# A two-layer diffusion step with top-2 experts on one core: expert rows weighted on the way out of PSUM, the second gather summed by its transfer, and TensorE fillers with a halved shift in the router

## What is computed

```python
def _moe(h, m, P):
    logits = jnp.einsum('nd,de->ne', xf, P['router'][m], preferred_element_type=jnp.float32)
    probs = jax.nn.softmax(logits, axis=-1)
    top_p, top_i = lax.top_k(probs, TOP_K)
    top_p = top_p / jnp.sum(top_p, axis=-1, keepdims=True)
    gates = jnp.sum(jax.nn.one_hot(top_i, N_EXPERTS, dtype=jnp.float32) * top_p[..., None], axis=1)
    for e in range(N_EXPERTS):
        y = y + gates[:, e:e + 1].astype(xf.dtype) * _swiglu(
            xf, P['moe_w_gate'][m, e], P['moe_w_up'][m, e], P['moe_w_down'][m, e])
# in _layer:  x = x + gf * f      and after the last layer:  y = _rmsnorm(x, final_norm_g)
```

## Time and profile before

| | us |
|---|---|
| median of 3 runs (1997.52 to 1998.13) | 1997.91 |
| the profiled execution's own time | 1998.52 |
| its span, first to last instruction | 1996.9 |
| TensorE busy in the span | 1971.9 (99%) |
| VectorE busy | 1530.0 (77%) |
| ScalarE busy | 1136.3 (57%) |
| GpSimd busy | 258.3 (13%) |

### The profile page before, as it was taken

How to read it: one execution, slowest core, us unless ns; L and a number is a source line. 1 busy time by engine, 2 the same in 40 slices (tenths; PEclk the granted TensorE clock), 3 DMA queues, 4 the chain that set the end, 5 groups by cost and what they waited for, 6 DMA issues and landing times. The chain is left out here.

```text
span 1996.9 us, 31145 instructions
## 1 busy us (share of the span) xinstructions
PE 1971.9 (99%) x11754; PEld 1763.4 (88%) x11754; DVE 1530.0 (77%) x1696; ACT 1136.3 (57%) x1383; POOL 258.3 (13%) x261
## 2 busy tenths in 40 slices
PE   8999999999999999999999999999999999999997
PEld 5898689999999999999879988888888888888885
DVE  5548678877767775765853589998998989989998
ACT  5217663322212223532865468777888887788775
POOL 1230100000000000132100056000000000000016
PEclk9999999999999999999999999999999999999999
DMA  9320433344444443422003499999999999999994
GB/s 336 99 86 6 149 117 127 127 138 153 153 149 143 152 135 98 128 67 74 1 1 74 174 346 374 385 386 386 386 384 384 386 386 383 381 385 385 385 378 190
DMA packets 265150, 448.21 MB, mean 224 GB/s; under 512 B 15104, under 2 KB 156384, under 8 KB 264896
## 3 DMA queue, kind: packets, MB, share of 16 engines
q1 hardware_dynamic: 244496, 378.37, 53.9%
q0 software_dynamic: 18688, 66.27, 9.1%
q10 hardware_dynamic: 1872, 2.26, 0.3%
HBM read 431.34 MB, written 16.64 MB: 224 GB/s over the span
## 5 line engine op out<-in xcount | busy, mean ns | idle before, releaser
L2102 DVE TENSOR_TENSOR w_lo<-mraw,w_hi 128x1792 fp32r<-128x1792 f32 (+2 forms) x306 | 643.7, 2116 | 80.6 <-ACT w_hi L1381 79.0
L1381 ACT ACTIVATE w_hi<-mraw 128x1792 fp32r<-128x1792 f32 (+2 forms) x306 | 541.4, 1775 | 166.0 <-PE ps L2788 161.6
L2786 PE MATMUL ps<-w_hi,xs_lo 128*128 128x448 f32 (+1 forms) x816 | 309.6, 379 | 0.7 <-DVE xs_lo L2107 0.7
L2788 PE MATMUL ps<-w_hi,xs_hi 128*128 128x448 f32 (+1 forms) x816 | 304.9, 374 | 0.0
L2787 PE MATMUL ps<-w_lo,xs_hi 128*128 128x448 f32 (+1 forms) x816 | 304.5, 373 | 0.0
L1503 DVE TENSOR_TENSOR sub_lo<-zone,sub_hi 128x1024 fp32r<-128x1024 f32 (+2 forms) x112 | 129.4, 1157 | 117.1 <-ACT sub_hi L1036 116.7
L1036 ACT ACTIVATE sub_hi<-zone 128x1024 fp32r<-128x1024 f32 (+2 forms) x112 | 109.2, 977 | 176.8 <-PE ps L2378 93.7
L2786 PEld LDWEIGHTS ps<-w_hi,xs_lo 128*128 128x128 f32 x816 | 153.2, 188 | 24.9 <-DVE w_lo L2102 6.4
L2788 PEld LDWEIGHTS ps<-w_hi,xs_hi 128*128 128x128 f32 x816 | 153.2, 188 | 19.2
L2787 PEld LDWEIGHTS ps<-w_lo,xs_hi 128*128 128x128 f32 x816 | 153.4, 188 | 17.8
L2363 PE MATMUL ps<-f_hi,sub_lo 128*128 128x320 f32 x704 | 162.2, 312 | 0.0
(11 more groups left out here) (360 smaller groups left out, 3653.0 us busy)
## 6 DMA issues: line engine op xcount, KB each, us to landing
mraw<-in_moe_w_down SPq DMA_DIRECT2D x68, 1024.0 KB, 8.9
mraw<-in_moe_w_up SPq DMA_DIRECT2D x68, 896.0 KB, 8.3
mraw<-in_moe_w_gate SPq DMA_DIRECT2D x68, 896.0 KB, 8.4
in_cos<-in_w_mods POOLq DMA_DIRECT2D x72, 512.0 KB, 3.6
mraw<-in_moe_w_gate SPq DMA_DIRECT2D x34, 1024.0 KB, 7.1
mraw<-in_moe_w_up SPq DMA_DIRECT2D x34, 1024.0 KB, 8.2
mraw<-in_moe_w_down SPq DMA_DIRECT2D x34, 768.0 KB, 8.5
zone<-in_w_in SPq DMA_DIRECT2D x13, 1024.0 KB, 5.2
```

The costliest lines, as they stand in the source:

```text
L1381: nc.scalar.activation(w_hi[:, n % SPLITS, a], mraw[:, n % MRING, a], ACT.Copy).then_inc(w_hi_ready, 1)
L2102: nc.vector.tensor_tensor(w_lo[:, n % SPLITS, a], mraw[:, n % MRING, a], w_hi[:, n % SPLITS, a].bitcast(f32), ALU.subtract).then_inc(w_spl ...
L2786: nc.tensor.matmul(out, a_lo, b_hi, start=start, stop=False)
L2788: return nc.tensor.matmul(out, a_hi, b_hi, start=False, stop=stop)
```

## The change

1. **Weights in the token line.** VectorE writes each token's weight into word 1 of its line, so there are two tables (`token_line`), both loaded by GpSimd, and VectorE waits for them (`no_tokens` at 64) before it writes. The scatter carries the weight to the slot's line.
2. **Rows weighted leaving PSUM.** GpSimd loads the line of slot s (`slot_info_in`) as the first thing in its loop body. VectorE waits for `info_in` and multiplies by `slot_weight` where it copied. In the last slot the weight goes into `latent_y` and `last_rows`.
3. **Gathers.** One zero row is added to `yslots`, to which rows of the last slot point. The first gathers of all tiles are issued, then the second ones with `compute_op=add` onto the first, each after the first has landed. They use fewer ring places, so they wait for pieces 9 and 10 of the last slot, and the final gain row is loaded earlier.
4. **Gating on VectorE.** No weighing is left on ScalarE or VectorE; VectorE multiplies each tile by the gate row, and the prompt's last-slot rows too. GpSimd computes nothing in the tail.
5. **GpSimd ahead of its loop.** `row_at` takes three operations, not ten. `hot` is still fifteen, without the weight.
6. **Router.** TensorE gets two fp32 matmuls of 512 columns with an unused result. The first tile's shift is made in two halves, and TensorE waits for the first half alone.

```diff
@@ build, GpSimd
-            pool.dma_start(token_i[:], d["token_i"]).then_inc(no_tokens, 16)
+            for c in range(2):
+                pool.dma_start(token_line[c][:], d["token_i"]).then_inc(no_tokens, 16)
             pool.wait_ge(rows_ready, 1)
-            pool.wait_ge(no_tokens, 32)
+            pool.wait_ge(no_tokens, 64)
...
-            rows, in_last, local, keep, step = rv[:, 1:3], rw[:, 0:2], rw[:, 2:4], rw[:, 4:6], rw[:, 6:9]
-            link(nc.gpsimd.tensor_scalar(in_last, rows, float(P * (SLOTS - 1)), None, ALU.is_ge))
-            link(nc.gpsimd.tensor_scalar(local, rows, -float(P * (SLOTS - 1)), None, ALU.add))
-            link(nc.gpsimd.tensor_scalar(keep, in_last, -1.0, 1.0, ALU.mult, ALU.add))
-            nc.gpsimd.tensor_tensor(keep, keep, rv[:, 9:11], ALU.mult)
-            link(nc.gpsimd.tensor_tensor(step[:, 2], rv[:, 2], rv[:, 1], ALU.subtract))
...
+            nc.gpsimd.tensor_scalar(local, rows, -float(P * (SLOTS - 1)), None, ALU.add)
+            link(nc.gpsimd.tensor_scalar(at, rows, float(P * (SLOTS - 1)), None, ALU.min))
+            nc.gpsimd.tensor_copy(row_at[:], at)
             pool.drain().then_inc(row_at_ready, 1)
             for t in range(TT):
-                link(nc.gpsimd.tensor_scalar(hot[:, t], iota_row, local[:, 0, t:t + 1], rv[:, 9, t:t + 1], ALU.is_equal, ALU.mult))
-                link(nc.gpsimd.tensor_scalar(hot_part, iota_row, local[:, 1, t:t + 1], rv[:, 10, t:t + 1], ALU.is_equal, ALU.mult))
+                nc.gpsimd.tensor_scalar(hot[:, t], iota_row, local[:, 0, t:t + 1], None, ALU.is_equal)
+                link(nc.gpsimd.tensor_scalar(hot_part, iota_row, local[:, 1, t:t + 1], None, ALU.is_equal))
                 link(nc.gpsimd.tensor_tensor(hot[:, t], hot[:, t], hot_part, ALU.add))
             pool.drain().then_inc(hot_ready, 1)
 
+            def slot_info_in(s):
+                pool.dma_start(slot_info[:], slot_tokens[bass.ds(s * P, P), 0:16]).then_inc(info_in, 16)
+
             with pool.Fori(0, SLOTS - 2) as s:
+                slot_info_in(s)
                 pool.wait_ge(xs_in, 16 * (s + 1))
...
+            for c in range(2):
+                for t in range(TT):
+                    if t in (1, 3) and c == 0:
+                        pool.wait_ge(w_split, NPC * (SLOTS - 1) + MRING + (t + 1) // 2)
+                    rows_at = bass.IndirectOffsetOnAxis(ap=row_at[:, c, t:t + 1], axis=0)
+                    if c:
+                        pool.wait_ge(gathered[t], 16)
+                        pool.indirect_dma_start(out=picked(t), out_offset=None, in_=yslots, in_offset=rows_at,
+                                                compute_op=ALU.add).then_inc(gathered[t], 16)
+                    else:
+                        pool.indirect_dma_start(out=picked(t), out_offset=None, in_=yslots, in_offset=rows_at).then_inc(gathered[t], 16)
@@ VectorE
+                if t == 0:
+                    nc.vector.tensor_tensor(htok[:, 0, 0:512], htok[:, 0, 0:512], shift_for[0][:, 0:512], ALU.add).then_inc(first_row_half, 1)
+                    nc.vector.tensor_tensor(htok[:, 0, 512:1024], htok[:, 0, 512:1024], shift_for[0][:, 512:1024], ALU.add).then_inc(htok_ready, 1)
+                    return
...
+            dve.wait_ge(no_tokens, 64)
             for c in range(2):
-                step(nc.vector.tensor_tensor(rv[:, 9 + c], rv[:, 5 + c], rv[:, 8], ALU.mult))
+                step(nc.vector.tensor_tensor(token_line[c][:].bitcast(f32)[:, :, 1], rv[:, 5 + c], rv[:, 8], ALU.mult))
...
+            def gate_rows_of(t):
+                dve.wait_ge(gathered[t], 32)
+                if t == 0:
+                    dve.wait_ge(gates_in, 32)
+                nc.vector.tensor_tensor(picked(t), picked(t), gate_row[t // (TT - 1)], ALU.mult).then_inc(rows_gated, 1)
...
-                nc.vector.tensor_copy(ybuf, ps[:, 3072:4096]).then_inc(y_evac, 1)
+                dve.wait_ge(info_in, 16 * (s + 1))
+                nc.vector.tensor_scalar(ybuf, ps[:, 3072:4096], slot_weight, None, ALU.mult).then_inc(y_evac, 1)
...
+            update(0)
+            dve.wait_ge(y_half, 2)
+            nc.vector.tensor_tensor(y_prompt, y_prompt, gate_row[1], ALU.mult).then_inc(prompt_y_gated, 1)
@@ TensorE
+            pe.wait_ge(htok_scaled, 3)
+            for _ in range(2):
+                nc.tensor.matmul(ps[:, o:o + N_LAT], ones[:], x_t[:, 0, 0:N_LAT], start=True, stop=True)
...
+                    if t or half:
+                        pe.wait_ge(htok_ready, t + 1)
+                    else:
+                        pe.wait_ge(first_row_half, 1)
```

More of the change, by code:

```diff
@@ L658, in build @@
         hot_ready, hot_turned, hot_out, row_at_ready = (sem(n) for n in ("hot_ready", "hot_turned", "hot_out", "row_at_ready"))
-        first_weighed, both_weighed, y_half = (sem(n) for n in ("first_weighed", "both_weighed", "y_half"))
+        y_half, info_in, first_row_half = sem("y_half"), sem("info_in"), sem("first_row_half")
         y_out, kv_out = sem("y_out"), sem("kv_out")
@@ L993, in _ @@
             pool.wait_ge(etr_done, 2 + G_ETR + 5 * (SLOTS - 2) + TR_OF["xb"] + 1)
-            for t in range(TT):
-                if t:
-                    pool.wait_ge(w_split, NPC * (SLOTS - 1) + MRING + t)
-                for c in range(2):
-                    pool.indirect_dma_start(
-                        out=picked(t, c), out_offset=None, in_=yslots,
-                        in_offset=bass.IndirectOffsetOnAxis(ap=row_at[:, c, t:t + 1], axis=0)).then_inc(gathered[t], 16)
-            pool.wait_ge(gates_in, 32)
-            for t in range(TT):
-                if t == TT - 1:
-                    pool.wait_ge(y_half, 2)
-                    nc.gpsimd.tensor_tensor(y_prompt, y_prompt, gate_row[1], ALU.mult).then_inc(prompt_y_gated, 1)
-                pool.wait_ge(both_weighed, t + 1)
-                nc.gpsimd.tensor_tensor(picked(t, 0), picked(t, 0), gate_row[t // (TT - 1)], ALU.mult).then_inc(rows_gated, 1)
+            for c in range(2):
[9 more added lines that the diff above has]
+                        pool.indirect_dma_start(out=picked(t), out_offset=None, in_=yslots, in_offset=rows_at).then_inc(gathered[t], 16)
         @block.scalar
@@ L1447, in last_rows @@
                 nc.scalar.activation(y_prompt[:, 512 * half:512 * half + 512], ps[:, 3072 + 512 * half:3584 + 512 * half],
-                                     ACT.Copy).then_inc(y_half, 1)
-            weigh_first(2)
-            weigh_first(3)
-            last_rows(0)
-            weigh_first(4)
-            last_rows(1)
+                                     ACT.Copy, scale=slot_weight).then_inc(y_half, 1)
+            act.wait_ge(info_in, 16 * SLOTS)
+            for half in range(2):
+                last_rows(half)
             act.wait_ge(ones_ready, 2)
@@ L2151, in expert_lo @@
                 if last:
[L2152 removed]
+                    gate_rows_of(0)
                 ahead(16)
@@ L2182, in latent_y @@
                 dve.wait_ge(y_left, SLOTS)
-                dve.wait_ge(gates_in, 32)
-                nc.vector.tensor_tensor(y_latent[:, a], ps[:, 3072:4096][:, a], gate_row[0][:, a], ALU.mult).then_inc(y_gated, 1)
-            weigh_both(1)
+                dve.wait_ge(info_in, 16 * SLOTS)
+                nc.vector.scalar_tensor_tensor(y_latent[:, a], ps[:, 3072:4096][:, a], slot_weight, gate_row[0][:, a],
+                                               ALU.mult, ALU.mult).then_inc(y_gated, 1)
+            gate_rows_of(1)
             latent_y(0)
-            weigh_both(2)
+            gate_rows_of(2)
             latent_y(1)
-            for t in range(3, TT):
-                weigh_both(t)
+            gate_rows_of(3)
+            gate_rows_of(4)
             def update(t):
@@ L2207, in last_norm @@
                     a = slice(w * n, w * n + w)
[L2208 removed]
+                    nc.vector.scalar_tensor_tensor(picked(t)[:, a], picked(t)[:, a], sums[:, 1, t:t + 1], fin_row[:, a],
                                                    ALU.mult, ALU.mult).then_inc(h_ready, 1)
[L2211 removed]
+            update(0)
+            dve.wait_ge(y_half, 2)
+            nc.vector.tensor_tensor(y_prompt, y_prompt, gate_row[1], ALU.mult).then_inc(prompt_y_gated, 1)
+            for t in range(1, TT):
                 update(t)
[L2213 to L2214 removed]
+                last_norm(t - 1)
             last_norm(TT - 1)
@@ L2894, in constants @@
     out["token_i"] = np.broadcast_to(np.arange(T, dtype=np.int32).reshape(TT, P).T[:, :, None], (P, TT, P))
+    out["zero_row"] = np.zeros((1, D_MODEL), np.float32)
     out["no_tokens"] = np.zeros((SLOTS * P, P), np.int32)
```

54 lines of the change are left out of this document (19 added, 35 removed).

## The result

The changed kernel takes 2003.92 us (median of 11 runs, 2002.58 to 2006.35); the kernel before, run beside it, 1998.42 (1997.52 to 2000.07). The ratio is 1.0027, with a 95% interval of 1.0019 to 1.0035: slower, by 5.5 us of the medians. The profiled execution took 2003.92 us, its span is 2002.3, where that of before is 1996.9: +5.4.

A forecast was written before the change was run, and what follows sets the result against it. TensorE bounds the expert loop, VectorE the end. Wait +11.1, clock +2.0, router 0 and tail -5.0 sum to +8.1 us, 2006.0 us on the median; eight times in ten 2000.5 to 2011.5.

The forecast's parts named there:

- The wait (+11.1): End of slot 0: VectorE's multiply waits for GpSimd's late first load, so TensorE gets piece 2 at 1222.1; +11.1 us.
- The two regimes: GpSimd's one-hot instructions: 8 run slowed beside VectorE until 1207.45, the last 7 unhindered in 5.2 us.
- The bounds, 1 and 21: Slot 0's pause: about 1 us if all 15 one-hot operations run unhindered, 21 if all take 2.15 us.
- my average of 2.15 us: Time per GpSimd one-hot operation beside VectorE's work, from all fifteen taking 32.3 us in the kernel before.
- The clock (+2.0): TensorE's restart after slot 0's pause: granted clock still low there, costing +2.0 us.
- The router (0, at most +1.1): Ahead of the experts: fillers save 1.7 us, the clock's fall moves to slot 0's first pieces, both swallowed; net 0.
- rival (e): Router: fillers fail and the clock falls at 1147.9 as before; sum unchanged, no chance of its own, within the main case.
- The tail (-5.0): After the last slot: weighings and GpSimd gatings removed, less 1.0 us for the second gather; -5.0 us, range -6.0 to -2.
- The best case, -6.0: Tail without any delay from the summed gathers: update 4 at 1983.8 instead of 1989.88; -6.0 us.
- 10.6 us of room: Tail: the fifth summed gather is issued at about 1962.3 and wanted at 1972.9, leaving 10.6 us.
- later than 9 us after issue: Tail: sign that the prediction is wrong, if the summed gathers land later than 9 us after issue.
- Rival (c): Tail: summed gathers run at half rate, so the tail gives -3 instead of -5, 2008 us in all; chance 0.2.

The follow-up runs named there:

- experiments 1 and 5: First: changed kernel with slot 0's load issued ahead of the one-hot instructions, 1995.18 us; second: that kernel plus three filler matmuls behind the gather matmuls, 1994.34 us.
- experiment 6: The kernel with the early load, with plain second gathers that overwrite instead of adding; 1993.68 us in one run.
- experiment 7's first kernel: The kernel with the early load, with the first tile's gate-row multiply moved behind weight piece 17 of the last slot; 1996.73 us in one run.

## Why the prediction was right

It said 2006.0 us, slower, for one reason: slot 0's new wait. Measured were 2003.92, and +5.5 on the kernel before where +8.1 was said. Sign, place and path are as predicted; the sizes are off by the terms below, and most of it is the wait. Point by point:

**The wait (+11.1): right in kind and place, 2.3 us too large.** The third piece of slot 1 begins at 1219.79, not 1222.1, which is +8.8 on the kernel before: 7.0 of pause, 1.6 that the router had already lost, and the rounding of the rows. Of the 2.3 us, 0.8 come from GpSimd's start (1185.98, not 1186.78), 1.2 from the fifteen instructions (20.5 us, not 21.7), 0.3 from the allowance to wake, for which no row of its own is seen. Behind the landing the working holds: 3.27 us to TensorE's restart, 3.2 predicted. The two regimes are both there, with other numbers: 1.56 us an instruction beside VectorE's work (the first twelve, 1190.16 to 1208.84), where I had taken 2.15, and 0.60, 0.60, 0.46 without it, where I had 0.82 from a comparison with a second scalar. At 1207.45 I had 8 of the 15 done, and 11 were. Both prices were too high; what kept the sum near is that VectorE was at work until 1209.1, 1.6 us longer than I had it. With the measured prices and VectorE still from 1207.45 on, the fifteen would have ended near 1209.7 (an estimate: eleven done, four at 0.58) and not at 1210.67, so about 1 us of the closeness is luck. The bounds, 1 and 21, were far wider than need be.

The rule of the Trainium skill (SBUF — State Buffer, "Who interferes with whom") that each side waits one whole instruction fits most rows better than my average of 2.15 us did: the two GpSimd instructions from 1204.74 and 1206.96 each end with one subtraction of VectorE's pair. But the one from 1193.85 takes 4.09 us across the whole pair from 1193.57. With the rule my sum would have been 2004.5, 0.6 above the median.

**The clock (+2.0): 1.3.** It fell during the pause, at about 1216.2 (0.58 in the mean of 1216 to 1217), and was back at 1223, 3.2 us behind the restart.

**The router (0, at most +1.1): right in the sum, wrong in its reasons.** The gather matmuls at full clock, their end (1155.4; 1155.1 said), the start of the experts set by the stores, and the fall of the clock at the experts: all seen. 1.6 us were lost, and the wait behind took them in, as said: counted to TensorE's restart there is no term left for them, but by the estimate above they held GpSimd up by about 1 us, inside the 0 to +1.1. But that the fillers keep the clock was argued, and the runs without them contradict it; rival (e), "the fillers don't do what they say", is true in another form than I wrote it. And the fall at the experts is not certain: it came in eight of ten profiles. Once the wait is gone, it reaches slot 15's result (1.2 us between experiments 1 and 5), and the end by 0.5 there.

**The tail (-5.0): -4.6, and -3.6 in the second profile.** The best case, -6.0, is what the kernel with plain second gathers shows: 5.8 (71.9 us from slot 15's result to the end before, 66.1 there). VectorE took up the first summed gather 7.6 us after its issue began, idled 1.05 us for it, and TensorE paused 0.76, where 1.0 was said (1.40 and 1.11 in the second profile). The step that failed is the fifth gather's "10.6 us of room". Moved by the 10.0 us of the loop, it would have been issued at 1972.3 and wanted at 1982.9. It was issued at 1975.22, since the five summed gathers take GpSimd longer than the plain ones of the earlier trace rows (2.61 and 3.34 us for the first two, where before 0.94 and 1.36; experiment 6 shows 2.6 us between plain and summed for the fifth's issue), and wanted at 1984.0: 8.8 us of room for the 9.0 that the chain has from issue to landing. It is the link on which the end hangs, and in other executions VectorE waits 0.6 to 1.2 us for it. The prediction called itself wrong if the summed gathers landed later than 9 us after issue. Here the latest is at that limit (8.8 us in the list of landings, 9.04 in the chain), in the second profile it is over it (9.8). The tail's range, -6.0 to -2, held all the same; the 9 us were the wrong sign to watch, since 10 us cost little more than 1 us at the end.

**Rival (c), half rate: true in kind, and cheaper than I priced it.** The Trainium skill (Collectives: The Full Stack, "The bandwidth ceiling") has it for the transfers of a ReduceScatter that the sum reads two sources, and that they run at about half the rate of a plain copy. The traces agree roughly: 179 to 188 GB/s at full share with the sum, 281 for the same gathers without it, 377 for the plain ones of the kernel before. I had priced it at 3 us against the best case; all that the sums cost, rate and issue together, is 1.3 us in the pair of profiles and 1.2 to 2.2 over all, of which 1.0 was in my sum.

The sum, then: 8.1 - 2.3 - 0.7 + 0.4 = 5.5, against 5.4 of the spans. With the second profile of each kernel it is 6.1 (2002.9 - 1996.8): the tail gives back 1.0 less there.

## What to carry to other kernels

When a wait for a transfer is added, look up where the transfer is issued the first time, not in the steady state: what its queue does ahead of its loop sets the price, and moving one issue ahead of that work can be worth more than the whole change. GpSimd instructions are as long as VectorE lets them be, so a block of them has two prices, one beside VectorE's work and one while it stands, and a new stall moves work from one to the other. For work whose cost depends on a clock that falls in some executions only, take several profiles before saying what keeps it up.

## What was unexpected of the hardware

- Behind the same pause (2.0 to 2.9 us, the gather matmuls before it and expert matmuls behind) the granted clock fell to half in eight of ten profiled executions and held in two, in one program once each way. A fall cost 1.3 to 1.6 us, once 2.7.
- How long the clock stays low behind a restart doesn't follow from the pause alone: 3.2 us behind 7.0 us of pause and 6.2 behind 14.4, but also 6.2 behind 2.90 (experiment 7's first kernel).
- The issue of a gather with a sum holds GpSimd 1.5 to 3.4 us (a plain one 0.9 to 3.0), and VectorE takes up the last of five queued ones 9.1 to 10.2 us after its issue in seven profiles. In the changed kernel the engines move 147 to 215 GB/s meanwhile.
- The same small load landed 4.9 us after its issue beside weight transfers, and 2.0 us after it while the queues were nearly idle (one load each).
- What decides whether the clock falls behind a pause of this length stays open.
